# Sums of squares for the norms: seven VectorE additions and one ones product in place of eight ones products

## The chip, the cores and the metric

One core of one Trainium2 chip. The time of a run is device microseconds from start to end of the program; lower is better. Three runs of the kernel before are given, and one execution of it was profiled.

## What is computed

A stack of two hybrid layers and a third block of another kind, on one sequence of 512 positions with 1024 features, all in f32. Each layer and the third block apply RMS norms to the running activations x; there are ten norms of the full width in all, and they are what this case is about:

```python
def rmsnorm(x, g):
    xf = x.astype(jnp.float32)
    y = xf * lax.rsqrt(jnp.mean(xf * xf, axis=-1, keepdims=True) + EPS)
    return y.astype(x.dtype) * g

for l in range(2):
    x = x + 0.5 * swiglu(rmsnorm(x, ffn1_norm[l]), ...)        # norm 3l
    x = x + hybrid_mixing(rmsnorm(x, mix_norm[l]), ...)        # norm 3l + 1
    x = x + 0.5 * swiglu(rmsnorm(x, ffn2_norm[l]), ...)        # norm 3l + 2
x = rmsnorm(x, final_norm)                                     # norm 6
x = x + mixer_2(rmsnorm_2(x, norm_mix_2), ...)                 # norm 7
x = x + swiglu(rmsnorm_2(x, norm_ffn_2), ...)                  # norm 8
out = rmsnorm_2(x, norm_final_2)                               # norm 9
```

## The kernel before

The activations lie transposed: feature rows on 128 partitions, eight tiles of 128 features (k = 0 to 7), 512 positions in the free dimension. So the mean over features runs over partitions and tiles. A norm goes through three engines:

- ScalarE squares x tile by tile into h, or into eight tiles of hid for norms 3l + 2 (lines 1067 to 1075). Each square waits for its tile of x (the semaphore x_upd) and raises sq_ready.
- TensorE multiplies the block of ones, 128x128, with each tile of squares and adds the eight products up in one PSUM bank (lines 448 to 453). The result has the sum over all 1024 features in every partition. sumsq_ready is raised once, by the last of them.
- ScalarE takes the square root of mean and eps (line 1075, to tmp 0, a part of the tile that the trace calls scr), VectorE its reciprocal (line 1408) and, tile by tile, x times gain times reciprocal (line 1411).

```python
            def norm(n, squares=h):

                for k in range(KD):
                    pe.wait_ge(sq_ready, 8 * n + k + 1)
                    last = mm(psum[:, 4, :], ones, squares[:, k, :], k == 0, k == KD - 1)
                last.then_inc(sumsq_ready, 1)
```

The large products are done in three parts each with rounded operands: a "high" copy by ScalarE (lines 1081, 1087) and a "low" rest by VectorE, whole minus high (line 1427). In norms 0 to 5 and 8 (norm_split, line 1433) VectorE splits the first block of weights in the ring buffer, which is called the ring split below, ahead of the reciprocal, and after it h tile by tile, which TensorE then takes up. Norms 6, 7 and 9 have no split.

Ahead of norms 1, 3, 4, 6 and 9 lies the down projection of a feed-forward part; VectorE adds its eight results to x in one go at its end (residual, line 1422). Ahead of norms 2, 5 and 8 lies an output projection whose eight results come one by one, each followed by its residual. Norm 7 squares the output of norm 6. Norm 3 is norm 0 of the second pass through the layer loop. Behind the square root of norm 7 ScalarE issues the loads of the second block's constants (lines 1224, 1225).

Every engine runs its own program in the order written; semaphores alone tie them together. All matmuls but a few are recorded at line 378, the helper mm. An f32 product has two MATMUL records.

Of the kernel before, what the change touches and what calls it, by code (L numbers as in the profile page):

```python
# [15 lines left out]
ALU = mybir.AluOpType  # L16
# [6 lines left out]
P = 128  # L23
S = 512
D = 1024
KD = D // P
# [18 lines left out]
MIX_ITEMS = len(MIX_COLS) + MIX_OUT  # L45
FFN_ITEMS = NJ + 6
LAYER_ITEMS = 2 * FFN_ITEMS + MIX_ITEMS
# [8 lines left out]
G_N1, G_NM, G_N2, G_QA, G_KVA, G_PS, G_FB, G_FIN = 0, 8, 16, 24, 26, 27, 29, 30  # L56
# [68 lines left out]
def build(nc, t_in, out):  # L125
    with ExitStack() as ctx:
        def sb(name, shape, dt=F32):
            return ctx.enter_context(nc.sbuf_tensor(name, shape, dt))

        def sem(name):  # L130
            return ctx.enter_context(nc.semaphore(name))

        psum = ctx.enter_context(nc.psum_tensor("psum", [P, 8, 512], F32))
# [3 lines left out]
        with ExitStack() as whole:  # L137
            h, ring, wdr, d2, hid = (whole.enter_context(nc.sbuf_tensor(n, shape, F32)) for n, shape in (
                ("h", [P, KD, S]),
                ("ring", [P, 2, SLOT]),  # L140
                ("wdr", [P, 2, HALF]),
                ("d2", [P, 22, S]),
                ("hid", [P, 24, S])))
# [6 lines left out]
        gains = sb("gains", [P, LAYERS, G_W])  # L150
# [10 lines left out]
        ones = cst[:, C_ONE:C_ONE + P]  # L161
# [13 lines left out]
        hid_squares = hid[:, 4:12, :]  # L175
# [18 lines left out]
        wdr_free = sem("wdr_free")  # L194

        sq_ready = sem("sq_ready")
        sumsq_ready = sem("sumsq_ready")
        rms_ready = sem("rms_ready")
        pads_zero = sem("pads_zero")
# [177 lines left out]
        def mm(o, w, r, start, stop):  # L377
            return nc.tensor.matmul(o, w, r, start=start, stop=stop, skip_group_check=True)  # L378
# [63 lines left out]
        def _(pe):  # L442
# [4 lines left out]

            def norm(n, squares=h):

                for k in range(KD):  # L450
                    pe.wait_ge(sq_ready, 8 * n + k + 1)
                    last = mm(psum[:, 4, :], ones, squares[:, k, :], k == 0, k == KD - 1)
                last.then_inc(sumsq_ready, 1)

            def mm3(o, w, r, start, stop):

                mm(o, w[0], r[0], start, False)
                mm(o, w[0], r[1], False, False)
                return mm(o, w[1], r[0], False, stop)
# [259 lines left out]
            for k in range(KD):  # L719
                pe.wait_ge(h_ready, 24 * LAYERS + k + 1)  # L720
                for o, c in firsts:
                    last = mm(o, w[:, k, c], h[:, k, :], k == 0, k == KD - 1)
# [3 lines left out]
            lo, hi = slice(0, 64), slice(64, 128)  # L726
# [20 lines left out]
            for g in range(2):  # L747

                o = product(f"av{g}")
                for t in range(NT):  # L750
                    for k in range(KD):
# [4 lines left out]
                        last = mm(o[:, t * P:(t + 1) * P], tok, w[:, k, g * P:(g + 1) * P], k == 0, k == KD - 1)  # L756
# [7 lines left out]
            for t in range(NT):  # L764
                last = nc.tensor.transpose(o[:, t * P:(t + 1) * P], hid[:, 18, t * P:(t + 1) * P], ident)
# [3 lines left out]
            for n in "ABKV":  # L769
                for t in range(NT):  # L770
                    o = product(f"t{n}{t}")
                    for p in range(3):
                        src = vfm[:, p, t * P:(t + 1) * P] if n == "V" else fm[n][:, p, t * P:(t + 1) * P]
                        last = nc.tensor.transpose(o[:, p * P:(p + 1) * P], src, ident)
# [48 lines left out]
            for g in range(3):  # L823
                for e in range(2):
                    for i in range(NT):
                        u = 8 * g + 4 * e + i
                        last = mm(psum[HD * e:HD * e + HD, g, i * P:(i + 1) * P],
                                  dstat[:, 2, u:u + 1].to_broadcast([P, HD]), ident, True, True)
# [204 lines left out]
            for n in range(2):  # L1033
                for m in range(2):
                    for k in range(2):
                        c = (W2_GV, W2_GG)[n] + k * 256 + m * P
                        last = mm(psum[:, 2 * n + m, :], mixw[:, c:c + P], hid[:, 22 + k, :], k == 0, k == 1)
# [4 lines left out]
            for m in range(KD):  # L1042
# [5 lines left out]
                for k in range(KD):  # L1048
                    c = slice((m % 2) * D + k * P, (m % 2) * D + (k + 1) * P)
                    last = mm3(psum[:, (m + 4) % 8, :], (out2_hi[i % 2][:, c], ring_lo[:, i % 2, c]),  # L1050
                               (merged_hi[:, k, :], merged_lo[:, k, :]), k == 0, k == KD - 1)
# [344 lines left out]
        def _(dve):  # L1396
# [5 lines left out]
            for k in range(KD):  # L1402
                dve.sem_inc(x_upd, 1)

            def norm(n, gain, into, split=None):

                dve.wait_ge(rms_ready, n + 1)
                nc.vector.reciprocal(tmp[:, 1, :], tmp[:, 0, :]).then_inc(rstd_ready, 1)  # L1408
                dve.wait_ge(rstd_ready, n + 1)
                for k in range(KD):  # L1410
                    nc.vector.scalar_tensor_tensor(out=into[:, k, :], in0=x[:, k, :], scalar=gain[:, k:k + 1],  # L1411
                                                   in1=tmp[:, 1, :], op0=ALU.mult, op1=ALU.mult)\
                        .then_inc(h_ready if into is h else x_upd, 1)
                    if split is not None and k:
                        split(k - 1)
                if split is not None:
                    split(KD - 1)
# [7 lines left out]
            def low(out_, whole, hi, made):  # L1425

                return nc.vector.tensor_tensor(out_, whole, hi, ALU.subtract).then_inc(made, 1)  # L1427

            def low_ring(s, cols=2 * KD * P, hi=None):
                hi = gu_hi[:, s, 0:cols] if hi is None else hi[s][:, 0:cols]  # L1430
                low(ring_lo[:, s, 0:cols], ring[:, s, 0:cols], hi.bitcast(F32), ring_split)

            def norm_split(n, n0, h0, gain, cols=2 * KD * P, hi=None):
                dve.wait_ge(ring_high, n0 + 1)
                low_ring(0, cols, hi)

                def split(k):
                    dve.wait_ge(h_high, h0 + k + 1)
                    low(h_lo[:, k, :], h[:, k, :], h_hi[:, k, :].bitcast(F32), h_split)

                norm(n, gain, h, split)

            def swiglu(f, n0, scale=0.5):
                with dve.Fori(0, NJ // 2) as jj:
                    for s in range(2):
                        j = 2 * jj + s
                        dve.wait_ge(ring_high, n0 + j + 2)
                        low_ring(1 - s)
                        dve.wait_ge(wd_high, f * NJ + j + 1)
                        low(wdr_lo[:, s, :], wdr[:, s, :], wd_hi[:, s, :].bitcast(F32), wd_split)  # L1450
                        dve.wait_ge(silu_ready, f * NJ + j + 1)
                        dve.wait_ge(ring_free, used(n0 + j))
                        nc.vector.tensor_tensor(hid[:, j, :], probs[:, s, :], psum[:, 2 + s, :], ALU.mult)\  # L1453
                            .then_inc(hid_ready, 1)
                        dve.wait_ge(hid_high, 2 * f * NJ + j + 1)
                        low(hid_lo[:, s, :], hid[:, j, :], hid_hi[:, s, :].bitcast(F32), hid_split)
                for k in range(NJ):
                    dve.wait_ge(hid_high, (2 * f + 1) * NJ + k + 1)
                    low(hid_lo[:, k % 2, :], hid[:, k, :], hid_hi[:, k % 2, :].bitcast(F32), hid_split)
                    if k in NEXT_ITEM:  # L1460
                        i = NEXT_ITEM[k]
                        dve.wait_ge(ring_high, n0 + NJ + i + 1)
                        low_ring(i % 2, DOWN_COLS[i])

                residual([(m, 4 + m, down_ready, 6 * f + m + 1) for m in range(3)]
                         + [(3, 7, wdr_free, used((f + 1) * NJ - 1))]
                         + [(4 + m, m, down_ready, 6 * f + m + 4) for m in range(3)]
                         + [(7, 3, ring_free, used(n0 + FFN_ITEMS - 1))], scale)
# [110 lines left out]
            with dve.Fori(0, LAYERS) as l:  # L1579
                norm_split(3 * l, l * LAYER_ITEMS, 24 * l, gains[:, l, G_N1:G_N1 + 8])  # L1580
                swiglu(2 * l, l * LAYER_ITEMS)
                norm_split(3 * l + 1, l * LAYER_ITEMS + FFN_ITEMS, 24 * l + 8, gains[:, l, G_NM:G_NM + 8],
                           KD * MIX_COLS[0], mix_hi)
                mixer(l)
                norm_split(3 * l + 2, l * LAYER_ITEMS + FFN_ITEMS + MIX_ITEMS, 24 * l + 16, gains[:, l, G_N2:G_N2 + 8])
                swiglu(2 * l + 1, l * LAYER_ITEMS + FFN_ITEMS + MIX_ITEMS)
            norm(3 * LAYERS, gains[:, 0, G_FIN:G_FIN + 8], x)

# [155 lines left out]
            for u in range(UNITS2 + 1):  # L1744
# [4 lines left out]
                if u >= 1:  # L1749
                    v = u - 1  # L1750
                    n = d_keys(v) * P
# [41 lines left out]
            for t in range(NT):  # L1793
                for name in VEC_STEPS:
                    for p in range(3):
# [14 lines left out]
                        if name == "N":  # L1810
# [4 lines left out]
                            last = masked("Nt", A[:, 256:512], mk16u)  # L1815
                        elif name == "M34":
                            after("M34b")
                            masked("Mak", B[:, 0:256], mkus)
                            last = masked("Mrb", B[:, 256:512], mkui)
                        elif name == "Y1":  # L1820
                            dve.wait_ge(rw_vec, done(VEC_STEPS, "N", t, p))
                            last = TT(two(cm(p, "Ya")), two(cm(p, "Nt")), mask2(ident), ALU.add)
                        elif name == "M5":
                            after("M5b")
                            last = masked("Mrk", B[:, 0:256], mkui)
                        elif name in ("Y2", "Y4", "Y8", "Y32", "XT"):
# [5 lines left out]
                            last = add(o, B[:, 0:256], other)  # L1832
                        elif name == "PT":
                            after("PTb")
                            last = TT(two(cm(p, "E2", P)), two(A[:, 0:P]),
                                      ident64.rearrange("p (o c) -> p o c", o=1).to_broadcast([P, 2, HD]), ALU.add)
                        elif name in ("Z0", "Z1"):
                            c = 2 * t + int(name[1])
                            after("S" + name[1] + "b")
                            if c < 7:  # L1840
                                last = TS(zst[:, p, (c + 1) % 4, :], A[:, 0:HD], dvec[:, p, c:c + 1], None, ALU.mult)
                            else:
                                last = nc.vector.engine_nop()
                        else:
                            after("Ub")
                            dve.wait_ge(rw_act, done(ACT_STEPS, "GW", t, p))
                            last = TT(cm(p, "N4", P), B[:, 0:P], cm(p, "N")[:, P:256], ALU.add)
# [352 lines left out]
```

## Time and profile before

| what | value |
|---|---|
| median of 3 runs | 3279.25 us (3278.21 to 3282.47) |
| profiled execution, span | 3278.0 us |
| TensorE matmul busy | 3097.5 us (94%), 13534 instructions |
| VectorE busy | 1331.2 us (41%), 1873 instructions |
| ScalarE busy | 1098.6 us (34%), 1570 instructions |
| GpSimd busy | 108.0 us (3%) |
| mean granted TensorE clock | 0.966 |

The profiled execution is known by its span, from the first to the last instruction; its time with what lies around it is not given apart, and the lowest of the runs is 0.2 us above the span. A granted clock of 1.00 is 2.4 GHz, 0.50 is 1.2 GHz. A row of a timeline gives the start and the length in us, the engine, the line, the operation, its output and inputs, and how many records were merged into it (x8); the length of a merged row reaches from the first start to the last end. In brackets stands the idle time of that engine ahead of the row and what ended it.

### The profile page before, as it was taken

Reading aid. Unit: us, or ns where it says so; the run is one execution under the profiler, and the core shown is the slowest. Engines: PE = TensorE matmul, PEld = TensorE weight load, DVE = VectorE, ACT = ScalarE, POOL = GpSimd, SP = SyncE. Lnnn points to the kernel's source line nnn. Section 1 sums busy time; section 2 is a strip of 40 time slices with the busy share of each in tenths; the row PEclk is TensorE's granted clock in tenths of the full one; section 3 lists DMA queues with packets and bytes.
Section 4 is the critical chain, followed back from the end, with each engine's and each line's share of the span. In section 5 each row is a group of like instructions: output and inputs, shape, how many; then the busy total and the mean of one; then the engine's idle time right before and its main releaser. Section 6 shows DMA issues by size and latency. Waiting matters only on the chain.

```text
span 3278.0 us, 35599 instructions
## 1 busy us (share of the span) xinstructions
PE 3097.5 (94%) x13534; PEld 2288.9 (70%) x13534; DVE 1331.2 (41%) x1873; ACT 1098.6 (34%) x1570; POOL 108.0 (3%) x130
## 2 busy tenths in 40 slices
PE   7999999999998999999989999889799999989997
PEld 5888775678886888866468888435488344678886
DVE  3333455443335333354643333444444753243334
ACT  3333433433334333332633333231322101233333
POOL 0000011000000000001000000000000430000000
PEclk9999999999999999999999999999599999999999
DMA  3222220022222222221012222211000121222221
GB/s 120 96 96 96 81 88 26 26 82 97 98 101 78 88 99 98 87 86 70 1 58 93 96 96 100 93 58 58 20 1 2 39 77 58 96 92 96 96 93 71
DMA packets 44712, 246.50 MB, mean 75 GB/s; under 512 B 5352, under 2 KB 5544, under 8 KB 20800
## 3 DMA queue, kind: packets, MB, share of 16 engines
q1 hardware_dynamic: 43200, 238.62, 20.9%
q10 hardware_dynamic: 1008, 6.24, 0.5%
q8 instruction: 68, 1.11, 0.1%
q0 software_dynamic: 400, 0.23, 0.0%
q14 instruction: 36, 0.29, 0.0%
HBM read 243.06 MB, written 2.10 MB: 75 GB/s over the span
## 4 chain that ended last, share of the span: by engine, by line
PE 88%; DVE 7%; ACT 2%; issue 2%; DMA 1%; DVEq 0%; ACTq 0%; SPq 0%
PE psum L378 87%; DVE scr L1408 1%; PE psum L634 1%; DVE stat L1536 1%; DVE scr L1544 1%; DVE ring_lo L1427 0%; DMA g2s<-in_g2s 0%; DVE scr L1802 0%; DVE h_lo L1427 0%; DVE scr L1858 0%; DVE hid L1525 0%; DVE scr L1521 0%; DVE scr L1523 0%; DVE h L1411 0%; DMA cst<-in_cst 0%
## 5 line engine op out<-in xcount | busy, mean ns | idle before, releaser
L378 PE MATMUL psum<-highs 128*128 128x512 f32 (+2 forms) x3872 | 1364.1, 389 | 56.1 <-DVE h_lo L1427 47.1
L378 PE MATMUL psum<-highs,ring_lo 128*128 128x512 f32 x2456 | 963.6, 392 | 0.0
L378 PEld LDWEIGHTS psum<-highs 128*128 128x128 f32 x3872 | 730.1, 189 | 221.8 <-DVE h_lo L1427 43.7
L378 PE MATMUL psum<-h_lo,highs 128*128 128x512 f32 x1952 | 766.6, 393 | 0.0
L1427 DVE TENSOR_TENSOR ring_lo<-ring,highs 128x2048 fp32r<-128x2048 f32 (+1 forms) x158 | 353.8, 2240 | 999.3 <-ACT highs L1096 873.6
L378 PEld LDWEIGHTS psum<-highs,ring_lo 128*128 128x128 f32 x2456 | 465.0, 189 | 99.2 <-issue 0.6
L1096 ACT ACTIVATE highs<-ring 128x2048 fp32r<-128x2048 f32 x110 | 210.9, 1917 | 667.4 <-DMA ring<-in_wgu 632.0
L378 PEld LDWEIGHTS psum<-h_lo,highs 128*128 128x128 f32 x1952 | 370.4, 190 | 79.1 <-issue 1.2
L378 PE MATMUL psum<-h,ring 128*128 128x512 f32 x704 | 313.2, 601 | 9.2 <-DMA cst<-in_cst 8.3
L378 PEld LDWEIGHTS psum<-h,ring 128*128 128x128 f32 x704 | 135.4, 194 | 185.1 <-issue 175.6
L1427 DVE TENSOR_TENSOR highs<-hid,highs 128x512 fp32r<-128x512 f32 x220 | 152.3, 692 | 244.9 <-ACT highs L1112 151.2
L378 PE MATMUL psum<-highs,wdr_lo 128*128 128x512 f32 x440 | 171.2, 389 | 0.0
L1104 ACT ACTIVATE highs<-hid 128x512 fp32r x110 | 69.5, 632 | 244.3 <-DVE hid L1453 243.0
L378 PE MATMUL psum<-d 128*128 128x128 f32 (+9 forms) x560 | 138.0, 376 | 4.4 <-ACT hid L1229 1.6
L1112 ACT ACTIVATE highs<-hid 128x512 fp32r<-128x512 f32 x110 | 69.5, 632 | 191.0 <-PE psum L378 191.0
L378 PE MATMUL psum<-hid 64*128 64x128 f32 (+9 forms) x528 | 106.6, 348 | 17.7 <-DVE d L1783 15.9
L378 PEld LDWEIGHTS psum<-d 128*128 128x128 f32 (+3 forms) x560 | 76.5, 177 | 53.5 <-issue 41.8
L1081 ACT ACTIVATE highs<-ring 128x2048 fp32r<-128x2048 f32 (+2 forms) x46 | 80.8, 1757 | 54.6 <-DMA ring<-in_wmix 50.1
L378 PEld LDWEIGHTS psum<-highs,wdr_lo 128*128 128x128 f32 x440 | 82.6, 188 | 17.1
L1357 ACT ACTIVATE scr<-psum 128x512 f32<-128x512 f32 x24 | 14.3, 597 | 232.9 <-PE psum L378 232.9
L378 PE MATMUL psum<-h,cst 128*128 128x512 f32 x128 | 62.4, 644 | 25.6 <-ACT h L1070 25.6
L1453 DVE TENSOR_TENSOR hid<-scr,psum 128x512 f32 x110 | 75.2, 684 | 21.9 <-PE psum L378 21.6
(329 smaller groups left out, 2814.0 us busy)
## 6 DMA issues: line engine op xcount, KB each, us to landing
ring<-in_wgu SPq DMA_DIRECT2D x110, 1024.0 KB, 5.3
ring<-in_wmix SPq DMA_DIRECT2D x24, 1536.0 KB, 6.3
wdr<-in_wd SPq DMA_DIRECT2D x110, 256.0 KB, 2.6
ring<-in_wd SPq DMA_DIRECT2D x25, 1024.0 KB, 4.8
ring<-in_wmix SPq DMA_DIRECT2D x20, 1024.0 KB, 4.8
mixw<-in_wsmall ACTq DMA_DIRECT2D x3, 1280.0 KB, 5.5
ring<-in_wd SPq DMA_DIRECT2D x5, 512.0 KB, 3.8
x<-in_x SPq DMA_DIRECT2D x1, 2048.0 KB, 11.0
```

Source lines behind the costliest of these rows:

```text
L378: return nc.tensor.matmul(o, w, r, start=start, stop=stop, skip_group_check=True)
L634: last = nc.tensor.transpose(psum[:, 3 + u % 2, t * P:(t + 1) * P], probs[:, u % 3, t * P:(t + 1) * P], ident)
L1081: nc.scalar.activation(into[:, 0:cols], ring[:, s, 0:cols], ACT.Copy).then_inc(ring_high, 1)
L1096: nc.scalar.activation(gu_hi[:, 1 - s, 0:2 * KD * P], ring[:, 1 - s, 0:2 * KD * P], ACT.Copy)\
L1104: nc.scalar.activation(hid_hi[:, s, :], hid[:, j, :], ACT.Copy).then_inc(hid_high, 1)
L1112: nc.scalar.activation(hid_hi[:, k % 2, :], hid[:, k, :], ACT.Copy).then_inc(hid_high, 1)
L1357: nc.scalar.activation(probs[:, q % 2, :], psum[:, 6 + q % 2, :], ACT.Sigmoid).then_inc(gate_act, 1)
L1408: nc.vector.reciprocal(tmp[:, 1, :], tmp[:, 0, :]).then_inc(rstd_ready, 1)
L1427: return nc.vector.tensor_tensor(out_, whole, hi, ALU.subtract).then_inc(made, 1)
L1453: nc.vector.tensor_tensor(hid[:, j, :], probs[:, s, :], psum[:, 2 + s, :], ALU.mult)\
L1536: nc.vector.tensor_reduce(stat[:, u % 3, 0:1], psum[:, u % 3, 0:n], AX.X, ALU.max, negate=True)\
L1544: nc.vector.tensor_scalar(probs[:, u % 3, 0:n], probs[:, u % 3, 0:n], stat[:, u % 3, 2:3], None, ALU.mult)\
```

## The change

TensorE waits for a new semaphore and issues one ones product in place of eight. VectorE first adds the seven other tiles of squares to tile 0, in place; each add waits for its square and for the add before. The adds stand behind the residuals and ahead of the ring split (norm_split) or of the reciprocal (norms 6, 7, 9).

```diff
         sq_ready = sem("sq_ready")
+        sq_added = sem("sq_added")
...
             def norm(n, squares=h):
 
-                for k in range(KD):
-                    pe.wait_ge(sq_ready, 8 * n + k + 1)
-                    last = mm(psum[:, 4, :], ones, squares[:, k, :], k == 0, k == KD - 1)
-                last.then_inc(sumsq_ready, 1)
+                pe.wait_ge(sq_added, 7 * n + 7)
+                mm(psum[:, 4, :], ones, squares[:, 0, :], True, True).then_inc(sumsq_ready, 1)
...
-            def norm(n, gain, into, split=None):
-
+            def add_squares(n, squares=h):
+
+                for k in range(1, KD):
+                    dve.wait_ge(sq_ready, 8 * n + k + 1)
+                    if k > 1:
+                        dve.wait_ge(sq_added, 7 * n + k - 1)
+                    nc.vector.tensor_tensor(squares[:, 0, :], squares[:, 0, :], squares[:, k, :], ALU.add).then_inc(sq_added, 1)
+
+            def norm(n, gain, into, split=None, added=False):
+
+                if not added:
+                    add_squares(n)
                 dve.wait_ge(rms_ready, n + 1)
...
-            def norm_split(n, n0, h0, gain, cols=2 * KD * P, hi=None):
+            def norm_split(n, n0, h0, gain, cols=2 * KD * P, hi=None, squares=h):
+                add_squares(n, squares)
                 dve.wait_ge(ring_high, n0 + 1)
                 low_ring(0, cols, hi)
...
-                norm(n, gain, h, split)
+                norm(n, gain, h, split, True)
...
-                norm_split(3 * l + 2, l * LAYER_ITEMS + FFN_ITEMS + MIX_ITEMS, 24 * l + 16, gains[:, l, G_N2:G_N2 + 8])
+                norm_split(3 * l + 2, l * LAYER_ITEMS + FFN_ITEMS + MIX_ITEMS, 24 * l + 16, gains[:, l, G_N2:G_N2 + 8],
+                           squares=hid_squares)
```

## Rows read from the trace of the kernel before

**Rows 1.** The page, chain that ended last, shares of the span by engine.
```profile
PE 88%; DVE 7%; ACT 2%; issue 2%; DMA 1%; DVEq 0%; ACTq 0%; SPq 0%
```

**Rows 2.** Tile cst and line 1408: count, shortest/median/longest ns, first and last start.
```profile
L378 PE MATMUL psum<-h,cst x128: 591/592/1223, 17.9 to 3261.2; 128*128 128x512 f32 x128
...
L1408 DVE RECIPROCAL scr<-scr x10: 3346/3353/3354, 28.0 to 3262.6; 128x512 f32<-128x512 f32 x10
```

**Rows 3.** Timeline of norm 1, by engine (VectorE, ScalarE, TensorE).
```profile
393.51 4.87 DVE L1422 SCALAR_TENSOR_TENSOR x<-psum,x 128x512 f32<-128x512 f32 x8
...
405.26 3.35 DVE L1408 RECIPROCAL scr<-scr 128x512 f32<-128x512 f32 x1 [2.97 <-ACT scr L1075]
408.76 1.41 DVE L1411 SCALAR_TENSOR_TENSOR h<-x,gains,scr 128x512 f32<-128x512 f32 x2 [0.15 <-DVE scr L1408]
...
394.23 4.81 ACT L1070 ACTIVATE h<-x 128x512 f32<-128x512 f32 x8 [1.36 <-DVE x L1422]
...
404.54 0.69 ACT L1075 ACTIVATE scr<-psum,cst 128x512 f32<-128x512 f32 x1 [2.57 <-PE psum L378]
...
397.47 7.03 PE L378 MATMUL psum<-h,cst 128*128 128x512 f32 x16
```

**Rows 4.** Timeline of VectorE in the second block: two dependent additions.
```profile
2144.99 0.69 DVE L1638 TENSOR_TENSOR scr<-scr 128x512 f32<-128x512 f32 x1
2145.71 0.69 DVE L1639 TENSOR_TENSOR scr<-scr,hid 128x512 f32<-128x512 f32 x1
```

**Rows 5.** Timeline of norm 2: last residual, square root.
```profile
667.32 0.69 DVE L1422 SCALAR_TENSOR_TENSOR x<-psum,x 128x512 f32<-128x512 f32 x1 [4.75 <-PE psum L378]
...
674.19 0.69 ACT L1075 ACTIVATE scr<-psum,cst 128x512 f32<-128x512 f32 x1 [2.20 <-PE psum L378]
```

**Rows 6.** Windows of TensorE: length, busy (records), granted clock, DMA share, GB/s.
```profile
31.00:32.00 1.00, 0.00 (x0) 1.00 0.00 0
32.00:33.00 1.00, 0.00 (x0) 0.80 0.00 0
...
410.00:411.00 1.00, 0.04 (x1) 0.50 0.00 0
```

**Rows 7.** Timeline of TensorE: the first f32 product of the second block.
```profile
2100.85 2.07 PE L378 MATMUL psum<-h,ring 128*128 128x512 f32 x2 [8.27 <-DMA cst<-in_cst]
```

**Rows 8.** Timeline of norm 0, at the kernel's start.
```profile
17.17 4.26 ACT L1070 ACTIVATE h<-x 128x512 f32<-128x512 f32 x8
...
17.85 9.36 PE L378 MATMUL psum<-h,cst 128*128 128x512 f32 x16 [17.85 <-ACT h L1070]
...
27.25 0.69 ACT L1075 ACTIVATE scr<-psum,cst 128x512 f32<-128x512 f32 x1 [2.50 <-PE psum L378]
```

**Rows 9.** Timeline of norm 7, by engine.
```profile
2082.08 5.39 DVE L1411 SCALAR_TENSOR_TENSOR x<-x,gains,scr 128x512 f32<-128x512 f32 x8
...
2083.54 9.04 PE L378 MATMUL psum<-h,cst 128*128 128x512 f32 x16 [5.61 <-ACT h L1070]
...
2092.62 0.69 ACT L1075 ACTIVATE scr<-psum,cst 128x512 f32<-128x512 f32 x1 [4.40 <-PE psum L378]
```

**Rows 10.** Timeline of norm 3, behind the loop's branch, by engine.
```profile
1039.57 4.87 DVE L1422 SCALAR_TENSOR_TENSOR x<-psum,x 128x512 f32<-128x512 f32 x8
...
1041.22 1.28 ACT L1070 ACT_TABLE_LOAD   x1 [2.30 <-issue]
...
1054.73 0.69 ACT L1075 ACTIVATE scr<-psum,cst 128x512 f32<-128x512 f32 x1 [4.63 <-PE psum L378]
...
1045.87 8.82 PE L378 MATMUL psum<-h,cst 128*128 128x512 f32 x16 [2.18 <-ACT h L1070]
```

**Rows 11.** Timeline of norm 8, by engine.
```profile
2875.82 0.69 DVE L1422 SCALAR_TENSOR_TENSOR x<-psum,x 128x512 f32<-128x512 f32 x1 [4.75 <-PE psum L378]
2883.11 2.29 DVE L1427 TENSOR_TENSOR ring_lo<-ring,highs 128x2048 fp32r<-128x2048 f32 x1 [6.60 <-ACT highs L1081]
...
2884.50 0.67 ACT L1075 ACTIVATE scr<-psum,cst 128x512 f32<-128x512 f32 x1
```

## The prediction

> **What bounds the kernel now.** I read the page first: the chain that ended last is 88% TensorE and 7% VectorE [rows 1]. So TensorE time is worth its full length, but only where TensorE really works; the change touches ten short places, the norms, and each has to be read by itself. The tile view gives what they consist of [rows 2]: 128 records of products with the ones block out of h (two records for each f32 product, eight products for each of eight norms; norms 2 and 5 read hid instead), and ten reciprocals of 3.35 us. In the timeline of norm 1 [rows 3] the reader is to see one serial path: the eight residual adds on VectorE end at 393.51 + 4.87 = 398.38, the sixteen records of the ones products run from 397.47 to 404.50, the square root starts at 404.54, the reciprocal at 405.26. Residuals and squares are nearly over when TensorE, until then busy with the down projection, takes up the first product, and it goes on from its last projection without a pause. So the norm's price today is 7.03 us of ones products, 16 records 0.43 us apart. Norm 4 repeats this, norms 6 and 9 too but for the ring split; in norms 2 and 5, at the end of a mixer, the last residual is issued alone [rows 5].
>
> **What the change puts in its place.** Seven adds, each of which reads the sum of the one before, then one product of two records, then the same square root. The adds stand behind all eight residuals in VectorE's order, so none of them starts while TensorE still works.
>
> The price of one dependent add is shown: two VectorE additions of 128x512 f32 in SBUF, the second waiting on a semaphore for the first, start 0.72 us apart and last 0.69 [rows 4]. I take 0.73 to allow for the second wait of each add: 6 x 0.73 + 0.69 = 5.07 us. The eight residuals start (4.87 - 0.69) / 7 = 0.60 us apart with records of 0.69, so an instruction that needs nothing of its predecessor starts 0.09 us before that one's record ends; the first add does. The Trainium skill (VectorE: DVE Perf Modes, The DRAIN you can't avoid) says that a semaphore between VectorE operations costs nothing extra. The rows have 0.03 us for it; by the page seven adds would be 4.84 us, 0.2 less per norm.
>
> The price of one product depends on TensorE's clock. At 2.4 GHz it is 0.43 + 0.59 = 1.02 us (spacing from rows 3, record length from rows 2); at 1.2 GHz a pair of the same shape after a pause took 2.07 us [rows 7]. Which one? In norm 1 TensorE would now pause from about 397.6 to 403.4, 5.8 us. Today it pauses from 404.50 to 410.95 and finds the clock at 0.50 [rows 6]. The slowest fall I find is in norm 0, whose products end at 27.21 [rows 8]: the clock is 1.00 from 31 to 32 and 0.80 in the next microsecond [rows 6], a fall at about 32.6, 5.4 us after the end. The new pause is just longer, so I take 2.07. The Trainium skill (TensorE: Matmul & The Clock Gate, Why this matters for your kernels) asks that TensorE not pause between bursts, since it then drops to half clock: a rule against this change, and the rows agree.
>
> A product starts 0.05 us after what it waits for, as the pair of norm 0 behind its first square (17.85 behind 17.17 + 0.63) [rows 8], and the square root 0.04 us after the product [rows 3]. Together: adds 5.07, 0.05, product 2.07, 0.04, that is 7.23 us from the start of the first add, 7.14 from the end of the last residual's record.
>
> Norm by norm, the square root after against before:
> - Norms 1, 4, 6, 9: 398.38 + 7.14 = 405.52 against 404.54 [rows 3], +0.98 each, +3.9.
> - Norms 2, 5: the last residual ends at 668.01, + 7.14 = 675.15 against 674.19 [rows 5], +0.96 each, +1.9. The eighth square is ready 0.7 us behind the residual, long before add 7 wants it.
> - Norm 7: its squares follow norm 6's own output, which VectorE finishes at 2082.08 + 5.39 = 2087.47. Today the products start at 2083.54, beside that output; the adds can't. 2087.47 + 7.14 = 2094.61 against 2092.62 [rows 9], +2.0. Behind this root ScalarE issues the loads of the second block's constants, and TensorE waited 8.27 us for them [rows 7]; so the 2.0 counts in full.
> - Norm 0: VectorE is idle and the squares come one by one, 0.52 apart; the second is ready at 17.17 + 0.52 + 0.63 = 18.32 and the adds, at 0.73, set the pace: 18.37 + 7.23 = 25.60 against 27.25 [rows 8], -1.6. Today's products take 9.36 us here and not 7.03, part of them at half clock, which is why there is a gain.
> - Norm 3: it follows the branch back of the layer loop. TensorE stood 2.18 us there and ScalarE 2.30, the latter for nothing that the profile shows, and half clock then made the products 8.82 us long [rows 10]. VectorE branches too; with the same 2.2 us its adds start at 1039.57 + 4.87 + 2.2 = 1046.64, the root at 1053.87 against 1054.73, -0.9.
> - Norm 8: the reciprocal waits for the ring split, and that for a weight load: split at 2883.11, root at 2884.50 [rows 11]. The adds end at 2876.51 + 4.98 = 2881.5, the product at 2883.6: 0, with 0.9 us to spare.
>
> Sum: 3.9 + 1.9 + 2.0 - 1.6 - 0.9 = **+5.3 us**. The ring split, now behind the adds, costs nothing: 2.29 us at most [rows 11], in norm 2 until 673.0 + 2.3 = 675.3, while the root ends at 675.15 + 0.69 = 675.8. With the product at full clock that cover would be gone in norms 2, 3 and 5. That TensorE issues 70 products fewer saves nothing else. After each norm it pauses today already and restarts at half clock; it will again.
>
> The sum is against the profiled span of 3278.0 us; the median of the runs shown, 3279.25, lies 1.25 above it and includes what stands around the span. The difference carries over: 3279.25 + 5.3 = **3284.5 us**, 0.16% up. A measurement of this kernel can tell about 0.2%, 6.6 us, from no change.
>
> **The rivals.**
> 1. *Full clock for the one product.* If the clock falls later than 5.8 us into the pause, the product takes 1.02. Norms 1, 4, 6, 9 come to -0.07 each; norms 2 and 5 to +0.3 (the split ends at 675.2, today's root is over at 674.9), norm 7 to +0.9, norm 3 to -1.5 (again by the split), norm 0 stays at -1.6, as TensorE has not run before it: -1.8, **3277.4 us**. For it: 5.4 is close to 5.8. Against it: in norm 3 a pause of 2.18 was enough. Chance 0.12.
> 2. *Clearly slower, on VectorE.* A dependent add costs 0.84 and not 0.73: behind the reciprocal a dependent instruction starts 0.15 us after the record's end [rows 3], where the two additions show 0.03. With 0.15, six gaps a norm grow by 0.11: 0.66, in nine norms 6.0 us, +11.3 in all, **3290.5 us**. It decides from a gap of about 0.065 us up, where the whole passes 0.2%. Two waits on each add speak for it, the row of the same operation against it. Chance 0.12.
> 3. *Chance in the clock.* Norms 0, 3 and 7 had half clock for a part of their old products, and each restart spends some time at it. Had norm 3's products run at full clock, as they may in other executions, its -0.9 becomes +0.9; the restarts can shift by some tenths each, either way: +3 to +9, centre **3286 us**. Chance 0.14.
>
> The forecast itself has 0.62.
>
> **How the numbers follow.** The ends of the unknown costs are 3277.4 and 3290.5. Leaving out a good half of each outer rival gives 3278.8 to 3289.5. Slower by over 0.2% needs more than +6.6: all of rival 2, four tenths of rival 3 and three tenths of the forecast, whose own spread I put at 2 us: 0.12 + 0.06 + 0.18 = 0.36. Faster by over 0.2% would need -6.6, which no case gives: 0.03 for what I have not seen. The rest is 0.61.
>
> **What would show it.** In the profile after: 70 more additions of 0.69 us on VectorE, 0.73 apart; one pair of records per norm, 2.07 us long, with the granted clock at 0.50; the root 1 us later against the last projection in norms 1, 2, 4, 5, 6, 9, 2 us later in norm 7, unmoved in norm 8, earlier in norms 0 and 3. TensorE's busy time falls by some 55 us with nothing to show for it, since that time becomes a pause. I am wrong if the adds start before the residuals end, if the pair lasts 1.02, or if the adds are spaced 0.8 or more.

## The result and the profile after

| | before | after |
|---|---|---|
| median, 20 runs each | 3277.65 us (3271.37 to 3286.54) | 3284.64 us (3278.73 to 3292.88) |
| ratio of after to before | | 1.0024, 95% interval 1.0015 to 1.0032 |
| profiled span | 3278.0 us | 3278.6 us |
| TensorE matmul busy | 3097.5 us | 3036.7 us |
| VectorE busy | 1331.2 us | 1378.1 us |

The change makes the kernel slower by 0.24%, 7.9 us by the ratio (5 to 10.5), 7.0 by the medians. TensorE does 61 us less work and VectorE 47 more, and the page of the profile after shows that the chain that ended last has shifted too: TensorE has 85% of it where it had 88%, VectorE 9% where it had 7% (compare [rows 1]). A new line of VectorE, 1410, the adds, has 1% of it.

```profile
PE 85%; DVE 9%; ACT 2%; issue 2%; DMA 1%; DVEq 0%; ACTq 0%; SPq 0%
```

Norm 1 after, timeline by engine, answers to [rows 3] (residual adds are now line 1431, square root 1074, reciprocal 1417):

```profile
391.00 4.87 DVE L1431 SCALAR_TENSOR_TENSOR x<-psum,x 128x512 f32<-128x512 f32 x8
395.79 5.04 DVE L1410 TENSOR_TENSOR h<-h 128x512 f32<-128x512 f32 x7
...
403.71 3.35 DVE L1417 RECIPROCAL scr<-scr 128x512 f32<-128x512 f32 x1 [1.17 <-ACT scr L1074]
...
402.99 0.69 ACT L1074 ACTIVATE scr<-psum,cst 128x512 f32<-128x512 f32 x1 [3.53 <-PE psum L379]
...
400.88 2.07 PE L379 MATMUL psum<-h,cst 128*128 128x512 f32 x2 [5.75 <-DVE h L1410]
```

The reader is to see the new serial path: residuals end at 395.87, seven adds in 5.04 us from 395.79, TensorE idle for 5.75 us, one pair of records in 2.07 us, the root at 402.99. From the residuals' end to the root it is 7.12 us; before it was 404.54 - 398.38 = 6.16. The windows of TensorE show why the pair is that long, the granted clock (the third column from the end) is 0.50:

```profile
401.00:402.00 1.00, 1.00 (x2) 0.50 0.00 0
```

In all ten norms the pair takes 2.07 or 2.08 us.

Norms 6, 7 and 9 after, outside the layer loop (VectorE's timeline; the first two rows are one chain of adds, of norm 6, behind residuals that end at 2066.59):

```profile
2066.50 4.66 DVE L1410 TENSOR_TENSOR h<-h 128x512 f32<-128x512 f32 x6
2071.63 0.69 DVE L1410 TENSOR_TENSOR h<-h 128x512 f32<-128x512 f32 x1 [0.46 <-DVE h L1410]
...
2083.90 5.46 DVE L1410 TENSOR_TENSOR h<-h 128x512 f32<-128x512 f32 x7
...
3254.78 5.45 DVE L1410 TENSOR_TENSOR h<-h 128x512 f32<-128x512 f32 x7
```

Here seven adds take 5.46 us, not 5.04, so they start 0.79 us apart, not 0.72, and 0.10 us lies between the end of one and the start of the next. In norm 6 one of these gaps is 0.46 us. The view of the line with the add's first wait, 1409, has an instruction of VectorE's own sequencer for it there, six a norm in four norms, which the layer loop's norms lack:

```profile
L1409 DVEq EVENT_SEMAPHORE  x24: 21/21/21, 2067.2 to 3259.5; - x24
```

Norm 3 after (compare [rows 10]): the residuals end at 1040.60, VectorE stands 2.74 us behind the loop's branch, and then the adds run as elsewhere. The row puts the idle time down to ScalarE's squares, but the second of them, which the first add waits for, was done at 1039.7.

```profile
1043.34 5.05 DVE L1410 TENSOR_TENSOR h<-h 128x512 f32<-128x512 f32 x7 [2.74 <-ACT h L1069]
```

The two profiled spans differ by 0.6 us only, far less than the medians. The roots of norms 1 and 2 are 269.65 us apart before and 267.46 after, though norm 2 is itself 0.94 longer; so 3.1 us came back in the mixer between them. Windows of TensorE, first before, then after, show it: of the mixer's steady projections and output products the kernel before ran a part at half clock.

```profile
461.00:470.00 9.00, 8.49 (x30) 0.81 0.30 113
620.00:630.00 10.00, 8.20 (x31) 0.83 0.00 0
```

```profile
461.00:470.00 9.00, 9.00 (x41) 1.00 0.22 87
620.00:630.00 10.00, 10.00 (x45) 1.00 0.00 0
```

A share of 0.81 in 9 us and of 0.83 in 10 us costs 1.7 us each, an estimate from these rows; the changed code is not near. One profile against one profile can't settle a difference of 7 us in this kernel, whose runs spread over 15.

Parts of the norms themselves differ from one execution to the next as well. Norm 3's ones products took 8.82 us in the profiles of the kernel before [rows 10] and of e8, but 7.13 in those of e6 and e10 below, where this part of the code is the same; norm 7's took 9.04 us, and 9.79 in e6.

### The profile page after: what moved, and what is told of

Same layout as the page of the kernel before. It is cut to its first block, busy times and chain, and to the rows that moved or that the text cites. A ratio compares the mean times of both kernels' runs of the same rounds, so it can differ in the third digit from the quotient of the medians.

```text
span 3278.6 us, 35449 instructions
## 1 busy us (share of the span) xinstructions
PE 3036.7 (93%) x13394; PEld 2258.4 (69%) x13394; DVE 1378.1 (42%) x1943; ACT 1098.2 (33%) x1570; POOL 107.9 (3%) x130
## 4 chain that ended last, share of the span: by engine, by line
PE 85%; DVE 9%; ACT 2%; issue 2%; DMA 1%; DVEq 0%; ACTq 0%; SPq 0%
PE psum L379 84%; DVE h L1410 1%; DVE scr L1417 1%; PE psum L633 1%; DVE stat L1546 1%; DVE scr L1554 1%; DMA g2s<-in_g2s 0%; DVE ring_lo L1436 0%; DVE x L1431 0%; DVE h_lo L1436 0%; DVE scr L1813 0%; ACT h L1069 0%; DVE x L1420 0%; DVE scr L1869 0%; DVE hid L1410 0%
## 5 line engine op out<-in xcount | busy, mean ns | idle before, releaser
L379 PE MATMUL psum<-h,cst 128*128 128x512 f32 x16 | 16.6, 1141 | 77.5 <-DVE h L1410 77.5
## 6 DMA issues: line engine op xcount, KB each, us to landing
x<-in_x SPq DMA_DIRECT2D x1, 2048.0 KB, 11.2
```

## The experiments

All times are against runs of the kernel before on the same chip; between two versions the ratios are compared. Where a sum of roots is given, it is the time from the end of the residuals (in norm 7 of norm 6's output, in norm 0 from the start of the first square) to the square root, in the version less in the kernel before, added over the ten norms of one profile each. For the changed kernel that sum is +7.2 us.

**e1: no adds.** The one product alone, behind the eighth square.

```diff
-                pe.wait_ge(sq_added, 7 * n + 7)
+                pe.wait_ge(sq_ready, 8 * n + 8)
                 mm(psum[:, 4, :], ones, squares[:, 0, :], True, True).then_inc(sumsq_ready, 1)
...
-                    add_squares(n)
```

> Leaves out the seven adds of every norm: TensorE waits for the eighth square and multiplies the ones block with tile 0 alone, so the sum of squares is that of one tile of eight. Theory (the change is worth what eight products less give and pays it back in dependent adds and a product at half clock): without the adds the square root no longer waits for TensorE but for ScalarE's own table load and ring copy. Root against before by the rows of before: norms 1 and 4 -2.6 us, 2 and 5 -2.2, 0 -2.5, 3 -4.6, 6 and 9 -4.0, 7 -2 to -3, 8 none: about -27 us against before. Rival (a longer pause of TensorE ahead of the restart costs time of its own, and this is what the changed kernel lost): the pause here is about as long, so a third or more of the 27 is missing and the restart at half clock lasts longer than in the kernel before.

Measured: 3251.79 us, ratio 0.9914 (0.9897 to 0.9932), -28 us. In norm 1 of this kernel the pair starts 1.45 us after the last projection, at full clock, and takes 1.12 us:

```profile
396.22 1.12 PE L379 MATMUL psum<-h,cst 128*128 128x512 f32 x2 [1.45 <-ACT h L1069]
405.40 0.79 PE L379 MATMUL psum<-highs 128*128 128x512 f32 x1 [8.06 <-DVE h_lo L1434]
```

The root is at 399.00, 1.7 us after the pair's end at 397.34: ScalarE has its copy and table load still to do. The sum of roots is -28.1 us. So seven products less are worth about 28 us in this kernel (22 to 34 by the interval), though the rows of the ones products are 62 us shorter (14.1 against 76.4); the adds, with the pause and the half clock that they bring, turn 28 us of gain into 8 of loss. The pause ahead of the restart, 8.06 us, is longer than before and nothing of the 28 is missing for it: the rival falls.

**e2: TensorE kept busy during the adds.**

```diff
+                pe.wait_ge(sq_ready, 8 * n + 1)
+                for _ in range(fill):
+                    mm(psum[:, 4, :], ones, cst[:, C_COS:C_COS + S], True, True)
                 pe.wait_ge(sq_added, 7 * n + 7)
```

> The changed kernel, with seven products of ones and a constant block (four in norms 0 and 3) that TensorE issues ahead of the one product, into the bank that the product then overwrites. It keeps TensorE busy during the adds; nothing else changes. Theory: the product's pair of records takes 1.02 us and not 2.07 at 2.4 GHz, the root comes 1.05 us sooner in norms 1, 4, 6, 7, 9 and, as the ring split then ends last, 0.6 sooner in 2 and 5; norms 0, 3 and 8 about as the changed kernel. Together 6 to 7 us less than the changed kernel, so within 1.5 us of the kernel before. Rival (the loss lies in the adds on VectorE alone, the clock plays no part): stays 5 to 9 us above before.

Measured: 3280.98 us, ratio 1.0004 (0.9995 to 1.0014), +1.3 us by the ratio, +3.1 by the medians. Norm 1 by engine:

```profile
398.35 5.04 DVE L1413 TENSOR_TENSOR h<-h 128x512 f32<-128x512 f32 x7
...
397.53 6.17 PE L379 MATMUL psum<-cst 128*128 128x512 f32 x14
403.54 1.03 PE L379 MATMUL psum<-h,cst 128*128 128x512 f32 x2
```

The adds are as long as they were, the pair takes 1.03 us, and by the ratios some 6.6 of the 7.9 us are gone, give or take 4. The rows are sharper: in norms 1, 2, 4 and 5 the root comes 6.18 us after the residuals, where the changed kernel has 7.12 and the kernel before 6.16 to 6.18. Half clock for one product per norm was most of the loss; with it away the adds and the seven products they replace cost the same. Two details went otherwise than expected. In norm 0 the root came 0.9 us sooner than in the changed kernel. In norm 3 four filling products were too few: TensorE paused 2.23 us behind them and the pair took 2.08 us.

**e3: one wait per add.**

```diff
                 for k in range(1, KD):
-                    dve.wait_ge(sq_ready, 8 * n + k + 1)
-                    if k > 1:
+                    if k == 1:
+                        dve.wait_ge(sq_ready, 8 * n + 8)
+                    else:
                         dve.wait_ge(sq_added, 7 * n + k - 1)
```

> The changed kernel, but the first add waits for all eight squares and the six others only for the add before. Theory (outside the layer loop each add has a wait of its own in VectorE's sequencer, which costs 0.06 us): the seven adds take 5.05 us in norms 6, 7, 8 and 9 as in the others, not 5.46; in norm 0 the first add starts 3 us later, in norm 7 0.7 us later, in norms 1, 4, 6, 9 it waits about 0.7 us for the last square. In all 2 to 5 us slower than the changed kernel. Rival (the 0.41 us come from code loading or from h as operand): the adds of norms 6 to 9 stay at 5.46.

Measured: 3290.99 us, ratio 1.004 (1.0027 to 1.0054), some 5 us slower than the changed kernel. Norm 9:

```profile
3271.97 5.05 DVE L1411 TENSOR_TENSOR h<-h 128x512 f32<-128x512 f32 x7 [0.69 <-ACT h L1069]
```

The chain is 5.05 us here and in norms 6, 7 and 8 as well, and the sequencer's instructions on the add's waits are gone outside the loop. Inside it the chain stays at 5.05. So the second wait, of constant value, costs 0.07 us an add outside the loop. The gap of 0.46 us in norm 6 is gone too. Why it was there stays open: e2 has it at the same add, and it went with the waits, which also moved the code.

**e4: rounded squares, eight products of one record.**

```diff
-                    pe.wait_ge(sq_ready, 8 * n + k + 1)
-                    last = mm(psum[:, 4, :], ones, squares[:, k, :], k == 0, k == KD - 1)
+                    pe.wait_ge(sq_ready, 8 * n + k + 2)
+                    last = mm(psum[:, 4, :], ones_r[:, :], hid_r[:, 16 + k, :], k == 0, k == KD - 1)
...
+            nc.scalar.activation(ones_r[:, :], ones, ACT.Copy).then_inc(sq_ready, 1)
...
-                    nc.scalar.activation(squares[:, k, :], x[:, k, :], ACT.Square).then_inc(sq_ready, 1)
+                    nc.scalar.activation(hid_r[:, 16 + k, :], x[:, k, :], ACT.Square).then_inc(sq_ready, 1)
```

> The kernel before, with the squares written rounded as f32r into eight free tiles and eight one-record products with a ones block of that type; no adds. Theory (the norm is bounded by the record count of the f32 product, 16 records 0.43 us apart; rounded products have 8 records 0.23 apart): the products hide behind the squares and the root is bounded by ScalarE as without adds, so -24 to -30 us against before, about the same as e1. Rival (only fewer products help, whatever their type): -10 us or less. The sum of squares is of values rounded to f32r.

Measured: 3254.23 us, ratio 0.9924 (0.9905 to 0.9943), -25 us (-31 to -19), as much as in e1, within the intervals. In norm 1 the eight products take 2.11 us from 395.69, where the f32 ones took 7.03, and the sum of roots is -29.5 us.

**e5: four pairs.** Half of the change.

```diff
+                for j in range(4):
+                    pe.wait_ge(sq_added, 4 * n + j + 1)
+                    last = mm(psum[:, 4, :], ones, squares[:, 2 * j, :], j == 0, j == 3)
...
+                for j in range(4):
+                    dve.wait_ge(sq_ready, 8 * n + 2 * j + 2)
+                    nc.vector.tensor_tensor(squares[:, 2 * j, :], squares[:, 2 * j, :], squares[:, 2 * j + 1, :], ALU.add).then_inc(sq_added, 1)
```

> Half of the change: VectorE adds the squares in four pairs that need nothing of each other, and TensorE adds up four products as the pairs come. Theory (what costs is the chain of dependent adds and the long pause with the product at half clock behind it, not the adds as such): in norm 1 TensorE pauses only 1.4 us, four products follow at 0.86 us each at full clock, and the root comes 1.9 us before that of the kernel before; likewise in norms 2, 4, 5, 6, 9; norms 0 and 3 gain 2 to 3 each, norm 7 loses 2 (its products run at half clock behind its long pause), norm 8 nothing. Together -10 to -16 us against before. Rival (any work of VectorE ahead of the products costs more than the products that it saves): 0 or slower.

Measured: 3265.82 us, ratio 0.9959 (0.9943 to 0.9975), -13 us. Norm 1:

```profile
397.24 2.48 DVE L1410 TENSOR_TENSOR h<-h 128x512 f32<-128x512 f32 x4
...
397.97 3.70 PE L379 MATMUL psum<-h,cst 128*128 128x512 f32 x8 [1.39 <-DVE h L1410]
```

Four independent adds, 0.60 us apart, run ahead of the products, which need 0.86 each; TensorE pauses 1.39 us and the granted clock stays at 1.00. The root comes 1.8 us sooner than before in norms 1, 2, 4, 5, 6 and 9; in norms 0, 3 and 7, where the four products took 6.2 to 6.5 us, it moved by -1.7, -0.8 and +2.0. Adds of the same shape on the same engine now gain. Which part of that is owed to their smaller number, which to their independence and which to the clock, this run does not separate.

**e6: TensorE kept busy behind the products,** in the kernel before.

```diff
                 last.then_inc(sumsq_ready, 1)
+                for _ in range(fill):
+                    mm(psum[:, 7, :], ones, cst[:, C_COS:C_COS + S], True, True)
```

> The kernel before, with seven products of ones and a constant block (nine in norm 8) behind the ones products of each norm that a split follows, into a bank that is free then. They keep TensorE busy during square root and reciprocal. Theory (each restart behind a norm spends 3 to 6 us at half clock, in both kernels alike, and this was no part of the change's price): the restart runs at 2.4 GHz, half of its present length at half clock is gained, 7 norms times about 2.2 us, -13 to -17 us against before. Rival (restarts are paced by VectorE's split of h, 1.27 us a tile, so the clock does not matter): -3 us to 0.

Measured: 3277.52 us, ratio 0.9994 (0.9983 to 1.0005): my theory is wrong. The clock did stay at 1.00 through the pause and the restart in all seven norms, but TensorE waits further on. Its first large product behind a norm is called the restart here; it uses the block of weights of the ring split, and the block after it in the ring buffer is called the second weight item. Timeline of norm 2, TensorE, first before, then e6; the first row of each is the restart, the second the first product with the second item:

```profile
680.61 0.80 PE L378 MATMUL psum<-highs 128*128 128x512 f32 x1 [6.46 <-DVE h_lo L1427]
...
693.82 0.50 PE L378 MATMUL psum<-highs 128*128 128x512 f32 x1 [0.21 <-DVE ring_lo L1427]
```

```profile
678.36 0.50 PE L378 MATMUL psum<-highs 128*128 128x512 f32 x1 [0.45 <-DVE h_lo L1429]
691.57 0.55 PE L378 MATMUL psum<-highs 128*128 128x512 f32 x1 [2.02 <-DVE ring_lo L1429]
```

Both are 13.21 us apart. VectorE ends the split of the second item then, whatever the clock; in norm 2 half clock at the restart was covered but for 0.2 us. It is much the same in norms 0, 3, 5 and 8, where TensorE waits 2.0 us in e6 too (0.0 to 0.5 us gained up to the second item). In norms 1 and 4, ahead of a mixer, the second item does come 1.2 and 1.4 us sooner. But in norms 2 and 5 the new wait of 2.0 us is followed by half clock again (in norm 2 the window 692 to 694 has 0.50), which takes back 1.6 us each (TensorE needs 12.6 us for the second item there, 11.0 in norms 0 and 3).

**e7: e4 with fillers** (ten, fourteen in norm 8).

> The kernel of e4 with ten such filling products behind the norm's own (fourteen in norm 8). Theory: both gains add up, as one shortens the norm and the other speeds up the restart: -25 and -15, about -38 us (-34 to -44) against before, where norm 3 gives a little of it back as its ten products may end late. Rival (the shorter norm leaves VectorE's split of h as the bound of the restart): -25 to -30 us. The sum of squares is of values rounded to f32r, as in e4.

Measured: 3249.98 us, ratio 0.9906 (0.9889 to 0.9922), -31 us (-36 to -26): near the rival, for the same reason as in e6, for in norms 0, 2, 5 and 8 TensorE waits 2.0 us for the second item here too.

**e8: e6 and an earlier copy of the second item.** ScalarE makes it right behind the root.

```diff
                 norm(n, early, squares)
+                second()
...
-                with act.Fori(0, NJ // 2) as jj:
+                pair(0, True)
+                with act.Fori(1, NJ // 2) as jj:
+                    pair(jj)
```

> The kernel of e6 (fillers in the pause, all else as before), and ScalarE makes the high copy of the second weight item right behind the square root, while it waits for the reciprocal, and not behind its eight copies of h. Theory from e6 (the restart at half clock is covered by the split of the second weight item, which ends 13.2 us after the restart in both kernels, so full clock only made TensorE wait 2.0 us for it): that wait goes, 1.5 to 2.2 us in each of the five norms ahead of a feed-forward part, little in norms 1 and 4: -8 to -13 us against before. Rival (the next thing is as late: table load, down weights or the first hidden tile): -2 to -5 us.

Measured: 3261.01 us, ratio 0.9946 (0.9932 to 0.996), -18 us; more than I had worked out. Norm 2, the second item:

```profile
685.58 0.39 PE L378 MATMUL psum<-highs 128*128 128x512 f32 x1
```

It starts without a wait, 11.02 us after the restart at 674.56. My sum had only the waits of 2.0 us in five norms. The half clock behind that wait in norms 2 and 5 of e6 is gone too, and norms 1 and 4, where I had put little, gain 1.8 and 2.0 us against before.

**e9: e7 with the earlier copy.**

> The kernel of e7 (rounded squares and fillers) with the same earlier copy of the second weight item. Theory: e7's -31 us and 7 to 11 more, -38 to -42 against before. Rival as in e8: -32 to -35. The sum of squares is of values rounded to f32r, as in e4.

Measured: 3237.12 us, ratio 0.987 (0.9851 to 0.9888), -43 us (-49 to -37), at the upper end of what I had worked out. The second item comes 11.0 to 11.3 us after the restart. This is the fastest version and beats both kernels.

**e10: the earlier copy alone,** no fillers.

> The kernel before with the earlier copy of the second weight item alone, no fillers. Theory (half clock at the restart and the late split of the second item cover each other, so that either alone gains next to nothing and both together gained 17 us in e8): the restart at half clock lasts and takes up what the earlier split frees; TensorE's wait of 0.2 us in front of the second item goes, -1 to -5 us against before. Rival (most of the gain of e8 is the earlier copy): -12 us or more.

Measured: 3276.55 us, ratio 0.9985 (0.9971 to 0.9998), -5 us. So -2 (-6 to +2) and -5 (-10 to -1) us apart, -18 (-22 to -13) together: each had been the other's cover. The rows agree. TensorE's time from the restart behind a norm to the second weight item (found as the 49th record) is:

| kernel | norms 0, 2, 3, 5, 8 | norms 1, 4 | less than before, seven norms |
|---|---|---|---|
| before | 13.2 to 13.7 us | 13.0, 13.2 us | |
| e6, fillers | 13.1 to 13.2 us | 11.8, 11.8 us | 3.9 us |
| e10, earlier copy | 12.4 to 13.7 us | 12.8, 12.6 us | 2.8 us |
| e8, both | 11.0 to 11.1 us | 11.2, 11.2 us | 16.0 us |

## Why the prediction was right

Direction, size and range held: 3284.5 forecast, 3284.64 measured, inside 3278.8 to 3289.5. That the two medians agree to 0.1 us is chance: I reckoned from a median of 3279.25, and 20 runs give 3277.65; the step was forecast as +5.3 and measured as +7.0 to +7.9. It fell just over the 0.2% that I had set, where I had 0.61 for "same" and 0.36 for "slower".

- *Dependent adds, 5.07 us.* Right inside the loop: 5.04 and 5.05. Outside, with two constant waits, 5.46, which e3 traced to the second wait. That is a part of rival 2: the gap of 0.10 us lies above its point of decision, 0.065, and below its 0.15, but in four norms only, three of them on the path: +0.4 each. The spacing of 0.79 is also just short of the 0.8 that I had named as a sign of being wrong.
- *The product at half clock, 2.07 us.* Right: 2.07 and 0.50 in the rows; e2 shows its worth, 0.94 us in a norm like norm 1. Rival 1 is refuted in every norm: behind the pauses of 5.74 to 15 us, and at TensorE's start in norm 0, the pair always took 2.07 or 2.08.
- *Root after the residuals in norms 1, 2, 4, 5.* Forecast +0.98 and +0.96, measured 7.12 against 6.16 and 6.18: +0.96 and +0.94.
- *Norms 6, 9, 7.* Forecast +0.98, +0.98, +2.0. Measured from the end of VectorE's work ahead: norm 6 2074.49 - 2066.59 = 7.90 against 6.16, +1.7; norm 9 7.53 against 6.16, +1.4; norm 7 7.55 against 5.15, +2.4. The terms were short by the second wait and, in norm 6, by the gap.
- *Norm 0.* Forecast -1.6, measured -1.6 (25.67 against 27.25). *Norm 3.* Forecast -0.9, measured 9.95 against 10.29, -0.3: VectorE stood 2.74 us at the branch, not 2.2. *Norm 8.* None, as forecast; the root still waits for ScalarE, with 0.3 us to spare and not 0.9.
- Summed with the measured terms: 3.8 + 1.7 + 1.4 + 2.4 - 1.6 - 0.3 = +7.4 us, which agrees with the medians. Missing in my sum were 2.1 us: 1.2 for the second wait, 0.4 for norm 6's gap (0.46 in place of 0.10), 0.5 at the branch. The terms of norms 3 and 7 hold for this pair of profiles: against e10's norm 3 (8.53 us from the residuals to the root) the changed kernel's 9.95 is +1.4, and against e6's norm 7 (5.91) its 7.55 is +1.6. That is a part of rival 3, so the close agreement of the sum is in part chance.
- *TensorE's busy time.* Forecast 55 us less, measured 61 on the page; the ones products' own rows are 55.7 less (76.4 to 20.7), and the rest lies elsewhere in the two executions.
- *Restart at half clock, no difference.* Right to within tenths: from the restart to the second item the changed kernel takes 13.2 to 13.9 us against 13.0 to 13.7, in one norm 0.5 us less, in another 0.7 more, 0.6 more in all seven. These are the tenths of rival 3. But my reason, that both kernels pay for the half clock, was mostly wrong: e6 shows that the kernel before pays for little of it, 3.9 us in seven norms. For the changed kernel no run shows it apart; its second item in norms 0, 2 and 3 comes 13.2 us after the restart as well. What also shifts, and what I had not thought of, is half clock in the mixers.
- *The ring split behind the adds, hidden.* Right: VectorE still waits 1.17 us for the root in norm 1, and 0.7 in norm 2, where it was closest.

## What to carry to other kernels

Count what an engine's removed work is worth from the wait that ends last without it: of 62 us of products only about 28 were on the path, and a serial chain on another engine, with the pause that it brought, cost more. A reduction split so that the two engines work side by side (e5) gained where the full replacement lost. Two latenesses that cover each other look worthless one by one; when a sound gain measures zero, look for the next wait that took its place, and try the two together.

## What had not been expected

- Outside a loop, a second wait of constant value on a VectorE instruction became a sequencer instruction of its own and cost 0.07 us in a dependent chain; in the loop, with values from registers, the second wait cost nothing that the rows show.
- Rounded f32r products of 128x512 come 0.23 us apart with one record each, f32 ones take two records 0.43 us apart: in norm 1 eight of the first took 2.11 us from the first start to the last end, eight of the second 7.03.
- Filling TensorE's pauses kept the clock at 1.00 through the pause and the restart in seven norms of e6 and moved the time by 2 us, which can't be told from no change (-6 to +2 us); in two of the seven the longer wait behind the restart brought half clock back.
